# Turning raw tokens before their RMS scale is known, and placing the modulation halves among the projection tiles

## What is computed

```python
def modulation(cvec, w_mod, b_mod):
    m = jax.nn.silu(cvec) @ w_mod + b_mod          # 1024 -> 6 * 1024
    return jnp.split(m[:, None, :], 6, axis=-1)

def trunk_layer(x, mod, shift_fn, s0_f, s0_b, lp):
    shift1, scale1, gate1, shift2, scale2, gate2 = mod
    hn = rmsnorm(x, lp['norm_mix_w']) * (1.0 + scale1) + shift1
    proj = hn @ lp['w_in']                          # 1024 -> 4480 columns
    ...                                             # pooling branch, two RWKV-7 scans, merge gates
    x = x + gate1 * mixed
    hn2 = rmsnorm(x, lp['norm_ffn_w']) * (1.0 + scale2) + shift2
    return x + gate2 * moe(hn2, lp), sf, sb         # 32 experts, top 4
```

## Time and profile before

| | |
|---|---|
| time, median of 3 runs | 1224.13 us (1222.58 to 1224.42) |
| time of the profiled execution | 1221.81 us |
| its span (first to last instruction) | 1220.0 us |
| PE busy | 1177.7 us, 97% of the span, 7087 matmul passes |
| DVE, ACT, POOL busy | 31%, 16%, 3% |
| DMA | 464.37 MB, 381 GB/s over the span |
| chain that ended last | PE 74%, DMA 22%, DVE 3% |

### The profile page before, as it was taken

The page is one execution under the profiler, slowest core; times in us unless marked ns, Lnnn a source line. Parts: engine busy times, 40 slices in busy tenths (PEclk is TensorE's granted clock), DMA queues, the critical chain, the costliest instruction groups (busy, mean ns, idle before and its releaser), DMA issues.

```text
span 1220.0 us, 17466 instructions
## 1 busy us (share of the span) xinstructions
PE 1177.7 (97%) x7087; PEld 557.1 (46%) x7087; DVE 382.9 (31%) x860; ACT 192.4 (16%) x363; POOL 41.6 (3%) x89
## 2 busy tenths in 40 slices
PE   6999999999999999999999999899999999999996
PEld 5777888987333333333333333333333333333333
DVE  2587984253421111122212211311112222122112
ACT  2350214201211111111211111111111111111002
POOL 5000210100000000000000000000000000000000
PEclk9999999999999999999999999999999999999999
DMA  9999230699999999999999999999999999999996
GB/s 331 325 380 354 71 112 34 209 393 405 385 429 429 428 429 428 428 429 429 428 429 428 427 407 427 427 428 430 429 428 429 427 427 430 429 429 428 429 427 256
DMA packets 73354, 464.37 MB, mean 381 GB/s; under 512 B 8375, under 2 KB 35662, under 8 KB 48094
## 3 DMA queue, kind: packets, MB, share of 16 engines
q1 hardware_dynamic: 70160, 458.12, 91.6%
q0 software_dynamic: 1504, 4.75, 1.1%
q10 hardware_dynamic: 1646, 0.86, 0.2%
HBM read 462.37 MB, written 1.34 MB: 380 GB/s over the span
## 4 chain that ended last, share of the span: by engine, by line
PE 74%; DMA 22%; DVE 3%; issue 1%; ACT 1%; ACTq 0%; DVEq 0%; SPq 0%
PE bank L1461 28%; DMA ring<-in_expert_w_gu 21%; PE bank L1578 12%; PE sums L809 5%; PE sums L1590 3%; PE sums L733 2%; PE sums L1265 2%; PE sums L1338 2%; PE sums L821 2%; PE bank L1373 2%; PE bank L1410 2%; PE sums L745 1%; PE bank L1558 1%; PE sums L945 1%; PE bank L709 1%
## 5 line engine op out<-in xcount | busy, mean ns | idle before, releaser
L1461 PE MATMUL bank<-ring,gate 128*64 128x512 f32 x1992 | 442.6, 599 | 14.5 <-DMA ring<-in_expert_w_gu 14.5
L1461 PEld LDWEIGHTS bank<-ring,gate 128*64 128x64 f32 x1992 | 139.9, 138 | 312.3 <-issue 282.1
L1578 PE MATMUL bank<-ring,gate 128*64 128x512 f32 x960 | 212.6, 595 | 3.3 <-DVE gate L2454 1.3
L2444 DVE TENSOR_SCALAR gate<-bank 128x512 f32<-128x512 f32 x31 | 21.4, 692 | 368.9 <-PE bank L1461 368.9
L1578 PEld LDWEIGHTS bank<-ring,gate 128*64 128x64 f32 x960 | 68.4, 137 | 126.8 <-issue 126.4
L1936 ACT ACTIVATE corr<-gate 128x512 f32<-128x512 f32 x31 | 19.5, 629 | 636.0 <-DVE gate L2444 636.0
L2460 DVE TENSOR_TENSOR corr<-bank,spare 128x512 f32<-128x512 f32 x31 | 21.4, 691 | 221.7 <-PE bank L1578 221.7
L1590 PE MATMUL sums<-corr,kk 64*128 64x512 f32 x248 | 61.6, 615 | 0.0
L1373 PE MATMUL bank<-qr,vt 128*64 128x512 f32 x248 | 58.5, 592 | 0.0
L809 PE MATMUL sums<-hnT,ring 128*128 128x256 f32 x256 | 56.4, 380 | 0.0
L809 PEld LDWEIGHTS sums<-hnT,ring 128*128 128x128 f32 x256 | 48.2, 190 | 7.1 <-issue 0.4
(11 more groups left out here) (440 smaller groups left out, 1048.1 us busy)
## 6 DMA issues: line engine op xcount, KB each, us to landing
ring<-in_expert_w_gu SPq DMA_DIRECT2D x122, 2048.0 KB, 19.3
ring<-in_expert_w_down SPq DMA_DIRECT2D x61, 2048.0 KB, 19.4
ring<-in_w_mod SPq DMA_DIRECT2D x16, 1024.0 KB, 9.9
ring<-in_w_in SPq DMA_DIRECT2D x13, 1024.0 KB, 10.4
ring<-in_w_mod SPq DMA_DIRECT2D x16, 512.0 KB, 9.9
ring<-in_expert_w_gu SPq DMA_DIRECT2D x5, 1024.0 KB, 18.4
ring<-in_w_in SPq DMA_DIRECT2D x9, 512.0 KB, 9.4
ring<-in_w_o SPq DMA_DIRECT2D x3, 1024.0 KB, 8.5
```

The lines of the kernel that those rows point to most:

```text
L1461: last = mm(b[h * SLOTS:(h + 1) * SLOTS, :], xg[:, 2 * (u % 2) + i, u // 2, :], w(u, i, j, h), start=False, stop=(u == GU_UNITS - 1 and i ...
L1578: last = mm(DN[h * SLOTS:(h + 1) * SLOTS, :], actT[:, i, u, :], w(GU_UNITS + u, i // 2, i % 2, h), start=(u == 0 and i == 0), stop=(u == D ...
```

## The change

1. **Raw turns.** PE turns each token tile as soon as the tokens have landed, with sixteen transposes against the identity, ahead of the wait for `rows_a`. The wide matmul on line 694 goes, and so do the sixteen scaling matmuls.
2. **The scale.** PE multiplies a matrix of ones with each diagonal, which gives the reciprocal root mean square of each token in all partitions (bank 2). ACT copies that to `junk` (a slot of the ring) ahead of its ten transfers. DVE multiplies the four banks with it on their way to `hnT`, bank 7 first. The modulation of both tiles then works in place in `hnT`.
3. **Places of the modulation.** Quarter 0's two halves follow each other with nothing between. The first half, the second half and the turn of the next quarter stand after tiles 5, 6 and 7 in quarter 0, after tiles 4, 5 and 6 in quarter 1, and after tiles 4, 4 and 5 in quarter 2 (before: 4, 4 and 5 in each).
4. **SP.** The six low-rank transfers are issued after chunk B0, not before it.

```diff
 # SP's queue
-        for c in range(8, AT["Q", 3] + 1):
+        for c in range(8, AT["B", 0] + 1):
             next_chunk(c)
...
-        for c in range(AT["Q", 3] + 1, AT["B", 1] + 1):
+        for c in range(AT["B", 0] + 1, AT["B", 1] + 1):
             next_chunk(c)
 # PE
         pe.wait_ge(S("consts_ready"), IDENT)
+        for s in range(NS):
+            pe.wait_ge(S(("x_in", "x1_in")[s]), 16)
+            for k in range(KT):
+                tr(turned(s, k), x[:, s, k * P:(k + 1) * P], ident[:])
         pe.wait_ge(S("rows_a_in"), 96)
         tr(banks[3][:, 0:96], rows_a[:], ident[0:96, 0:96]).then_inc(S("front_mm"), 1)
-        pe.wait_ge(S("x_in"), 16)
-        mm(banks[2][:, :], ident[:], x[:, 0, 0:512], start=True, stop=True)
-
-        def token_turn(s, some):
-
-            for k in some:
-                last = mm(turned(s, k), x[:, s, k * P:(k + 1) * P], xn[:, s, 0:P], start=True, stop=True)
-            return last
...
         for s in range(NS):
             pe.wait_ge(S("xn_ready"), s + 1)
-            last = token_turn(s, (5, 7))
+            last = mm(banks[2][:, s * T:(s + 1) * T], ones[:], xn[:, s, 0:P], start=True, stop=True)
         last.then_inc(S("front_mm"), 1)
-        for s in range(NS):
-            token_turn(s, (0, 1))
         pe.wait_ge(S("cpad_ready"), 1)
         pe.wait_ge(S("xn_ready"), 3)
-        mod_quarter(0, (0,))
-        for s in range(NS):
-            token_turn(s, (2, 3))
-        mod_quarter(0, (1,))
-        token_turn(0, (4, 6))
+        mod_quarter(0, range(2))
         quarter_turn(0)
-        token_turn(1, (4, 6))
         for c in range(4):
             for n in range(NQ):
                 part(n, c)
                 if c == 1 and n == 4:
                     pe.wait_ge(S("prb_ready"), 1)
-                if c < 3 and n == 4:
-                    mod_quarter(c + 1, range(2))
-                if c < 3 and n == 5:
+                if c < 3 and n == (5, 4, 4)[c]:
+                    mod_quarter(c + 1, (0,))
+                if c < 3 and n == (6, 5, 4)[c]:
+                    mod_quarter(c + 1, (1,))
+                if c < 3 and n == (7, 6, 5)[c]:
                     quarter_turn(c + 1)
 # ACT
         af(csig[:].rearrange("p s k -> p (s k)"), prm[:, 0:16], ACT.Sigmoid).then_inc(S("csig_ready"), 1)
 
+        act.wait_ge(S("front_mm"), AFTER["xnT"])
+        af(junk[:, 0, 0:TT], banks[2][:, 0:TT], ACT.Copy).then_inc(S("csig_ready"), 1)
         rows(rows_b, 0, r128(A["shift_mu"][0]), 15, "rows_b_in")
...
-                last = af(hnT[:, k, s * T:(s + 1) * T], turned(s, k), ACT.Identity,
+                last = af(hnT[:, k, s * T:(s + 1) * T], hnT[:, k, s * T:(s + 1) * T], ACT.Identity,
                           bias=moda[:, 0, k, s:s + 1], scale=moda[:, 1, k, s:s + 1])
 # DVE
-        dve.wait_ge(S("front_mm"), AFTER["xnT"])
-        v.tensor_copy(hnT[:].rearrange("p (k j) t -> p k j t", j=2)[:, 2:4, 1, :], banks[7][:, :].rearrange("p (k t) -> p k t", k=2)).then_inc(S("xn_ready"), 1)
+        dve.wait_ge(S("csig_ready"), 2)
+
+        def scaled(b):
+
+            j, g = (b - 4) // 2, (b - 4) % 2
+            return v.tensor_tensor(hnT[:].rearrange("p (k j) t -> p k j t", j=2)[:, 2 * g:2 * g + 2, j, :],
+                                   banks[b][:, :].rearrange("p (k t) -> p k t", k=2), bc(junk[:, 0, 0:TT], 2), MUL)
+
+        scaled(7).then_inc(S("xn_ready"), 1)
+        for b in (4, 6, 5):
+            step(scaled(b))
...
-                src = turned(s, k) if c < 2 else hnT[:, k, s * T:(s + 1) * T]
-                last = v.tensor_scalar(hnT[:, k, s * T:(s + 1) * T], src, moda[:, 1, k, s:s + 1], moda[:, 0, k, s:s + 1], MUL, ADD)
+                h = hnT[:, k, s * T:(s + 1) * T]
+                last = v.tensor_scalar(h, h, moda[:, 1, k, s:s + 1], moda[:, 0, k, s:s + 1], MUL, ADD)
             last.then_inc(S("hnd_ready"), 1)
 
+        last_of("xn_ready", 3)
         modulated(0)
```

## The result

Over 17 runs each, the changed kernel takes 1225.62 us (median; 1222.40 to 1228.95) and the kernel before 1222.85 us (1221.11 to 1224.71). The ratio is 1.0021, 95% interval 1.0015 to 1.0027, so the change costs 2.8 us by the medians, 1.8 to 3.3 by the interval. The forecast was +1.7 us and 1225.8 us. Ratios leave out slow executions, of which there was one: 1524.92 us at a mean granted clock of 0.749, among the eleven of the kernel with the old places.

What follows compares the result with a forecast made beforehand. The prediction took the front to be bound by PE's own chain of work, its shifts reaching the end. Head -2.5, turns +2.2 and clock +2.0 summed to +1.7 us on 1224.13, giving 1225.8 us; 8-in-10 range 1223.0 to 1228.4.

Steps and rivals of the forecast that it cites:

- The narrow range: Forecast's own range for the whole kernel: 1224.8 to 1226.6 us, from 3 to 5 us at the lower clock and handoffs.
- The head, -2.5: Ahead of the first tile: modulation starts at 10.9 and the first tile at 16.7, gaining 2.5 us.
- The covers: Before the first tile: ACT's transfers end 1.1 us before ACT is needed; DVE is free about 0.5 us ahead of turned sums.
- The turns, +2.2: Ahead of quarters 1 and 2: PE waits 1.55 and 0.68 us for turns no longer hidden by tiles, 2.2 us together.
- The halves themselves are the same passes in another place: nothing: Quarters' tiles: moving the modulation halves among them was claimed to cost 0 us beyond the waits for turns.
- The clock, +2.0: First tiles: PE's breaks ahead of them leave 4 us at the lower clock, losing 2.0 us.
- the second rival: Front tiles: standstills keep or bring the clock down, 8 us low, 1227.8 us; signs: second slow stretch or rise after 22; chance 0.28.
- SP, 0: Low-rank transfers behind B0: the last lands at 51.3, 3.0 us later, before the decay matmuls want it; no cost.
- One for one: From the decay matmuls on: a shift at 53.9 us should reach the kernel's end in full.
- The rule on transposes: Raw turns at the start: by the cited skill, transposes do not raise the clock; the sum stays at +1.7 us.
- The first rival: Front tiles: the clock is up when they start and stays up, sum -0.3 us, 1223.8 us; chance 0.20.

Runs made afterwards that it cites:

- the kernel with the old places: Changed kernel with the modulation halves and the turn back after tiles 4, 4 and 5 in every quarter; 1220.98 us, ratio 0.9986 to the kernel before.
- product held back: Changed kernel with GpSimd's 128x512 subtraction held until quarter 0 is modulated; 1225.96 us, ratio 1.0024 to the kernel before.
- old SP order: Changed kernel with the six low-rank transfers issued ahead of chunk B0 again; 1225.87 us, ratio 1.0025 to the kernel before.
- the 48 turns: Changed kernel with the sixteen raw turns made three times over, to see whether transposes raise the clock; one traced execution, no time given.
- new places alone: Kernel before with only the changed kernel's places of the modulation halves and turns; 1226.05 us, ratio 1.0032 to the unedited kernel before.
- The filling: Changed kernel with four unread 256-column matmuls, one behind the two with ones, three behind quarter 0's turn; 1222.85 us, ratio 1.0007 to the kernel before.
- with transposes: Changed kernel, modulation places as before the change, each unread matmul in PE's idle time at the start replaced by four 128x128 transposes; 1221.24 us, ratio 0.9987.
- places-only experiments: Changed kernel with the modulation places of before, ratio 0.9986; kernel before with the changed kernel's places, ratio 1.0032.
- the last kernel: Changed kernel with the modulation places of before, four unread matmuls at the start and seven in the last expert; 1219.54 us, ratio 0.9976 to the kernel before.
- places and filling together: Changed kernel with the modulation places of before (4, 4, 5) and four unread matmuls at the start; 1221.10 us, ratio 0.9981 to the kernel before.
- the split halves: Kernel before with the two modulation halves after tiles 3 and 4, turn after tile 5, in quarters 1 to 3; 1224.45 us, ratio 1.0012.
- Filling the last expert alone: Kernel before with only seven unread matmuls in the last expert; 1221.34 us, ratio 0.9991 to the unedited kernel before.

## Why the prediction was right, and where its terms were off

The sum was -2.5 + 2.2 + 2.0 = +1.7 us. Measured are +2.8 (1.8 to 3.3), so the forecast lies just below the interval. The sign and the three mechanisms stand; the first term held within the scatter of executions, the second was too small, the third a little too large. That the forecast time of 1225.8 us lies 0.2 us from the measured 1225.62 is luck: it was built on 1224.13, the median of three executions, which over 17 is 1222.85, and the 1.3 us too much there made up for the 1.1 us too little in the sum. The narrow range given with it, 1224.8 to 1226.6, is also 0.1 us lower than its own terms make it.

- **The head, -2.5.** From the vectors to the first tile it is 10.88 us in the trace of before and 7.8 to 8.2 in the three traces of the changed head with no long step and no filling (old places, product held back, old SP order); three further traces of the old head give 11.08, 10.98 and, where the clock rose sooner (at 12.25), 10.11. So the gain is 1.9 to 3.3 by the pair of executions. In the changed kernel's own trace it is 1.5, or 2.3 without the long step. Modulation at 10.9 and first tile at 16.7 were forecast; with vectors at 8.18 (old places) they came at 10.76 and 16.41. In the profiled execution of the changed kernel the first tile came at 18.55. The covers held: ACT's transfers end at 14.06 there and ACT is needed at 15.43; VectorE is free at 15.26 and its turned sums come at 16.29.
- **What moved it beside the change.** The turn of the vectors starts between 8.2 and 9.0 us in the five traces built on the kernel before, and between 8.2 and 9.4 in the eight built on the changed one (leaving out the 48 turns). The prediction took one execution's 8.28 as given. That is 1 us of scatter ahead of everything else; whether the change has a part in it is not known. The decay matmuls were forecast near 55.6 and came at 56.05 and 56.84 in the two other traces of this start and these places, and at 58.22 in the profiled one, with its late vectors and long step.
- **The turns, +2.2.** The waits were forecast at 1.55 and 0.68 and came at 1.46 and 0.66 (1.39 and 0.59 in the kernel before with the new places). The step that failed is "The halves themselves are the same passes in another place: nothing". Split from each other they make one more passage in quarters 0 and 1, 0.34 us each, and by the sum above each wait costs 0.16 beyond its length. The quarters grew by 3.1 us (new places alone) and 3.2 (changed kernel, after 1.7 for the clock).
- **The clock, +2.0.** All five traces of the changed start without filling, whatever their places, have exactly one low stretch of 3.41 us in quarter 0's tiles, and it costs 1.7 us (quarter 0 takes 13.16 with it and 11.48 without, at the new places). It came as the second rival had it in kind, the clock rising and falling back (up at 15.99, down at 19.41, and up again only at 22.82 in the changed kernel, a time that the prediction had named as that rival's sign), but with the forecast's price: one stretch in the tiles, no second. The filling shows the cause: in all four traces with PE's standstills filled, with matmuls or with transposes, the stretch is gone.
- **SP, 0.** 51.3 was forecast for the landing and 50.9 measured; undone, no difference.
- **The sum by its measured parts** is -2.3 + 3.2 + 1.7 = +2.6 us with the head of the changed kernel's own trace. With the 7.8 us of head in the two other traces of this start and these places it is +1.9, as the distance from the vectors to the decay matmuls says too (47.49 us in both, 45.60 before). That is the lower edge of the interval, so up to 0.9 us of the median is not laid to a part. The two places-only experiments agree: restored 0.9986, alone 1.0032, and their product 1.0018 lies in the interval of the whole.
- **One for one.** The middle, from the decay matmuls to the first gather, is 271.1 to 272.1 us in every trace but that of the last kernel (272.7, with its new wait of 1.1 us in it), so a shift at the front does arrive at the experts. It reaches the end only within the scatter of the next section, and that is enough to hide a front 1.3 us shorter, as in places and filling together.
- **The rule on transposes.** The prediction cited the Trainium skill ("TensorE: Matmul & The Clock Gate", Part 4, PE-mode transpose), by which transposes do not bring the clock up. Here the measurement decides against it, for fp32 transposes of 128x128: they did so in four traces (up at 7.43, 7.87, 8.20 and 10.65 with nothing else ahead). The first rival gained nothing from that, since without filling the clock fell again behind the standstills, and the sum did not use the rule.

## What to carry to other kernels

Starting an engine's chain earlier pays only as far as nothing behind it stands still. Keep as much independent work between a small transpose and its user as the way through the other engines takes, here two tiles of 0.88 us for 1.66. Do not split a run of small matmuls without need, since each passage to them and back costs PE 0.34 us here. Where PE stood for 1.2 and for 1.5 to 2.4 us before a dense stretch, four matmuls that nobody reads gave back 1.7 us. Before a change of 0.2% is judged from one trace, cut the trace at a point behind the change: here 3.4 of 7 us lay where the change does nothing.

## What the runs showed that was not expected

- The last expert runs at the lower clock for 0, 3.4 or 6.8 us by the execution. From the first gather to PE's end it is 887.5 to 888.1 us in five traces with none, 888.9 to 889.5 in four with 3.4, and 890.5 to 891.1 in three with 6.8. It occurs without the change: the split halves, built on the kernel before, have 3.4 us of it. But of the four traces built on the kernel before without filling there, only that one has it, and of the eight built on the changed kernel six. That the change makes it likelier was not tested. The mean granted clock speaks for no large part: it is 0.9890 over the 17 executions of the changed kernel and 0.9914 over those of the kernel before that ran beside the experiments, some 6 us more at the lower level, and the traces of the changed start without filling have 3.4 or 6.8 us of that at the front. Seven short matmuls in a wait of 1.9 us took it out of both traced executions, and the runs of the last kernel lie within 1.2 us, those of the kernel before within 3.6. Filling the last expert alone took about 1.1 us off the kernel before, and about 0.6 us off the kernel with old places and filling, by the ratios; neither step by itself is clear of noise.
- The lower clock can follow a rise closely: with the clock up at 7.43 or 7.87, after transposes, it was down by 10.9 and 11.3, up at 14.3 and 14.7 and down again by 17.7 and 18.1 (old SP order, product held back).
- A 0.16 us step of VectorE with both operands in SBUF is held by GpSimd's 1.26 us product of two operands until that is done, in all four traces in which the two meet in the front. A step with one operand in a bank is not, and GpSimd's instructions with one operand hold neither. This is read from traces; no run varied the operands.
